# A third attention unit with a score buffer of its own, and a softmax tail that runs one weight tile later

## What is computed

```python
scores = einsum('bnqkgd,bnjkd->bnkgqj', qb, kb) * (HEAD_DIM ** -0.5)
scores = where(valid, scores, NEG_INF)              # causal, window of 128
m = maximum(max(scores, -1), sink)
pexp = exp(scores - m)
probs = pexp / (sum(pexp, -1) + exp(sink - m))
out = einsum('bnkgqj,bnjkd->bnqkgd', probs, vb)     # 8 heads, 2 key/value heads
branches = einsum('bsrc,rcd->bsrd', stack([y_conv, y_pool, y_att]), w_branch)
merged = sum(sigmoid(gate_logits) * branches, axis=2)
```

## Time and profile before

| | us |
|---|---|
| median of three runs | 1214.61 |
| the profiled execution: device time | 1214.84 |
| its span between first and last instruction | 1213.3 |
| TensorE busy in it | 1196.4 (99%) |
| VectorE busy | 887.0 (73%) |
| ScalarE busy | 715.4 (59%) |
| granted TensorE clock, mean share of full speed | 0.998 |
| first product of tile 14 of the gate stage, first layer | 172.81 |
| the same, second layer | 635.89 |

### The profile page before, as it was taken

The page is one execution under the profiler, slowest core; times in us unless marked ns, Lnnn a source line. Parts: engine busy times, 40 slices in busy tenths (PEclk is TensorE's granted clock), DMA queues, the critical chain, the costliest instruction groups (busy, mean ns, idle before and its releaser), DMA issues.

```text
span 1213.3 us, 15342 instructions
## 1 busy us (share of the span) xinstructions
PE 1196.4 (99%) x5990; PEld 997.6 (82%) x5990; DVE 887.0 (73%) x812; ACT 715.4 (59%) x675; POOL 111.4 (9%) x134
## 2 busy tenths in 40 slices
PE   8999999999999999999999999999999999999997
PEld 5998788888888888998788888888888888888875
DVE  4777755655444457767755788998888988888996
ACT  5437444543443437336534577777777777777765
POOL 3620000200000001340000000001000000000301
PEclk9999999999999999999999999999999999999999
DMA  9955455665555555555455499999999999999970
GB/s 333 323 196 176 163 181 175 220 217 188 181 200 176 191 188 174 191 174 174 145 171 186 150 359 371 387 374 389 378 388 380 392 377 390 380 389 378 393 286 35
DMA packets 152457, 319.11 MB, mean 263 GB/s; under 512 B 6000, under 2 KB 41088, under 8 KB 152400
## 3 DMA queue, kind: packets, MB, share of 16 engines
q1 hardware_dynamic: 147632, 302.80, 71.0%
q0 software_dynamic: 4480, 14.51, 3.2%
q10 hardware_dynamic: 288, 1.05, 0.3%
HBM read 311.51 MB, written 6.82 MB: 262 GB/s over the span
## 4 chain that ended last, share of the span: by engine, by line
PE 91%; DVE 4%; ACT 3%; issue 1%; DMA 1%; SPq 0%; POOLq 0%; DVEq 0%; POOL 0%; ACTq 0%
PE ps L1960 24%; PE ps L1705 17%; PE ps L1707 17%; PE ps L1706 17%; PE ps L1947 11%; DVE split L1057 2%; ACT split L674 1%; PE ps L1927 1%; PE ps L1721 1%; DMA raw<-ple_w_proj_dram 1%; PE ps L1772 1%; PE ps L1832 1%; PE ps L1904 1%; PE ps L1783 0%; DVE X L1278 0%
## 5 line engine op out<-in xcount | busy, mean ns | idle before, releaser
L1057 DVE TENSOR_TENSOR split<-raw,split 128x2048 fp32r<-128x2048 f32 x272 | 623.1, 2295 | 202.8 <-ACT split L674 200.3
L674 ACT ACTIVATE split<-raw 128x2048 fp32r<-128x2048 f32 x274 | 524.8, 1916 | 259.1 <-PE ps L1707 187.7
L1960 PE MATMUL ps<-split,br 128*128 128x512 f32 x1344 | 317.4, 392 | 0.5 <-DVE split L1057 0.3
L1960 PEld LDWEIGHTS ps<-split,br 128*128 128x128 f32 x1344 | 249.5, 188 | 54.9 <-DVE split L1057 2.0
L1705 PE MATMUL ps<-split,hT 128*128 128x512 f32 (+1 forms) x600 | 234.5, 391 | 2.5 <-DVE hT L1105 1.2
L1707 PE MATMUL ps<-split,hT 128*128 128x512 f32 (+1 forms) x600 | 230.4, 384 | 0.0
L1706 PE MATMUL ps<-split,hT 128*128 128x512 f32 (+1 forms) x600 | 230.3, 384 | 0.0
L1947 PE MATMUL ps<-split,hT 128*128 128x512 f32 x672 | 159.6, 392 | 0.1
L1947 PEld LDWEIGHTS ps<-split,hT 128*128 128x128 f32 x672 | 124.8, 188 | 27.9 <-issue 1.6
L1705 PEld LDWEIGHTS ps<-split,hT 128*128 128x128 f32 x600 | 112.8, 188 | 29.0 <-DVE hT L1105 3.3
L1707 PEld LDWEIGHTS ps<-split,hT 128*128 128x128 f32 x600 | 112.7, 188 | 22.5
(11 more groups left out here) (283 smaller groups left out, 963.1 us busy)
## 6 DMA issues: line engine op xcount, KB each, us to landing
raw<-moe_w_gu_dram SPq DMA_DIRECT2D x96, 1024.0 KB
raw<-moe_w_down_dram SPq DMA_DIRECT2D x56, 1024.0 KB
raw<-w_in_dram SPq DMA_DIRECT2D x45, 1024.0 KB
raw<-ffn_w_gu_dram SPq DMA_DIRECT2D x28, 1024.0 KB
raw<-moe_w_gu_dram SPq DMA_DIRECT2D x32, 512.0 KB
raw<-ffn_w_down_dram SPq DMA_DIRECT2D x14, 1024.0 KB
raw<-w_branch_dram SPq DMA_DIRECT2D x12, 1024.0 KB
raw<-w_out_dram SPq DMA_DIRECT2D x8, 1024.0 KB
```

Source lines behind the costliest of these rows:

```text
L674: act.activation(buffer(t, 0), raw[:, t % RAW, :], ACT.Copy).then_inc(hi, 1)
L1057: dve.tensor_tensor(buffer(t, 1), raw[:, t % RAW, :], buffer(t, 0).bitcast(F32), ALU.subtract).then_inc(lo, 1)
L1960: ins = pe.matmul(ps[:, 5 if kind == "up" else 4, :], xe[:, sl, 4 * part + k, :], slot(t, sr, 512)[:, k, :], start=part + k + m == 0, stop ...
```

## The change

It does four things.

1. `scores_of(2)` is no longer the first half of `Y` but `upool[:, :, 16:]`. With that the wait for `pr_turned` ahead of unit 2's mask goes. Since `upool` is not contiguous over heads, scores are now addressed by head.
2. The six turns move from after tiles 5 to 10 to after tiles 6 to 11, and the six copies (`take_probs`) from tiles 6 to 11 to tiles 7 to 12.
3. The three products with the values move from after tiles 7, 9, 11 to after tiles 8, 10, 12.
4. `ATT_HALF` becomes 9 and `ATT_OUT` 13: `values_hi` and `values_lo` also move one tile on.

```diff
@@ -38,7 +38,7 @@
 
 
 
-ATT, ATT_HALF, ATT_OUT = 1, 8, 12
+ATT, ATT_HALF, ATT_OUT = 1, 9, 13
 ATT_UNITS = ((0, 0, HEADS, P), (1, 0, HEADS // 2, SEQ), (1, HEADS // 2, HEADS // 2, SEQ))
 
 CHAN_COLS = (1536, 1792, 512, 768, 1024, 1280, 0, 256)
@@ -367,7 +367,9 @@
 
         def scores_of(u):
 
-            return Y[:, u % 2, :]
+            if u == 2:
+                return upool[:, :, 16:]
+            return Y[:, u, :].rearrange("p (h n) -> p h n", n=ATT_UNITS[u][3])
 
         def probs_of(half):
 
@@ -775,7 +777,7 @@
                 _, _, nh, n = ATT_UNITS[u]
                 act.wait_ge(masked, 3 * l + u + 1)
                 for h in range(nh):
-                    s = scores_of(u)[:, h * n:(h + 1) * n]
+                    s = scores_of(u)[:, h, :]
                     act.activation(s, s, ACT.Exp, bias=nmx[:, u % 2, h:h + 1],
                                    accum_out=den[:, u % 2, h:h + 1])
                 act.activation(esk[:, u % 2, 0:nh], esk[:, u % 2, 0:nh], ACT.Exp).then_inc(exped, 1)
@@ -1189,9 +1191,7 @@
             def mask_scores(l, u):
                 _, h0, nh, n = ATT_UNITS[u]
                 dve.wait_ge(s_done, 3 * l + u + 1)
-                if u == 2:
-                    dve.wait_ge(pr_turned, 6 * l + 2)
-                s3 = scores_of(u).rearrange("p (h n) -> p h n", h=nh)
+                s3 = scores_of(u)
                 for s in range(2):
                     ins = dve.scalar_tensor_tensor(
                         out=s3[:, s:nh:2, :],
@@ -1527,8 +1527,8 @@
                         at = 3 * c + step
                         if at == ATT_HALF:
                             values_lo(l, 0)
-                        if 0 <= at - ATT - 5 < 6:
-                            take_probs(l, at - ATT - 5)
+                        if 0 <= at - ATT - 6 < 6:
+                            take_probs(l, at - ATT - 6)
                         for stage, late in ((scale_probs, 4), (mask_scores, 1)):
                             if at - ATT - late in (0, 2, 4):
                                 stage(l, (at - ATT - late) // 2)
@@ -1776,12 +1776,14 @@
 
             def att_turn(l, piece):
                 u, half = piece // 2, piece % 2
+                per = ATT_UNITS[u][3] // P
                 pe.wait_ge(probs, 3 * l + u + 1)
                 if piece:
                     pe.wait_ge(prT_ready, 6 * l + piece)
                 for i in range(4):
                     ins = pe.transpose(ps[:, 7, i * P:(i + 1) * P],
-                                       scores_of(u)[:, (4 * half + i) * P:(4 * half + i + 1) * P], ident[:, :])
+                                       scores_of(u)[:, (4 * half + i) // per, i % per * P:(i % per + 1) * P],
+                                       ident[:, :])
                 ins.then_inc(pr_turned, 1)
 
             def att_values(l, u):
@@ -2175,10 +2177,10 @@
                                 if b == 0:
                                     ins.then_inc(branch_done, 1)
                         ins.then_inc(tile_used, 1)
-                        if at - ATT - 6 in (0, 2, 4):
-                            att_values(l, (at - ATT - 6) // 2)
-                        if 0 <= at - ATT - 4 < 6:
-                            att_turn(l, at - ATT - 4)
+                        if at - ATT - 7 in (0, 2, 4):
+                            att_values(l, (at - ATT - 7) // 2)
+                        if 0 <= at - ATT - 5 < 6:
+                            att_turn(l, at - ATT - 5)
                         if at - ATT in (0, 2, 4):
                             att_scores(l, (at - ATT) // 2)
                         if at == 15:
```

## The result

| | before | changed |
|---|---|---|
| median, us (12 runs each) | 1214.44 | 1217.86 |
| lowest to highest | 1213.97 to 1215.24 | 1216.05 to 1219.46 |
| profiled execution: span | 1213.3 | 1216.7 |
| TensorE busy | 1196.4 | 1197.9 |

The ratio is 1.0026, 95% interval 1.0019 to 1.0033: the change costs 3.4 us (2.3 to 4.0 by the interval), where 2.5 were forecast. The time is inside the range of 1215.3 to 1218.7, and 0.2 us above the narrower one, 1216.1 to 1217.7, that the forecast gave itself. Two things in the table were not forecast: almost a microsecond more, and runs of the changed kernel that spread over 3.4 us, those of before over 1.3.

The account below looks back on a forecast made before the run. TensorE, busy 99% of the span, was taken to bound the kernel. A 2.18 us loss less a 0.95 us gain per layer, 2.46 us over both, moved the median from 1214.61 to 1217.1 us; range 1215.3 to 1218.7.

Parts of the forecast that it names:

- the narrower one: Range for the main forecast alone, 1216.1 to 1217.7 us: the stall's bounds less 0.95 us, twice; chance 82%.
- What bounds the kernel: TensorE is busy 99% of the span, so only its standing still or doing more can move the end.
- The gain: Gate stage: without unit 2's mask wait, TensorE's waits for the `sc` copy and the division go, 0.95 us per layer.
- The loss: Tile 14: TensorE waits for `values_hi`, queued behind tile 13's second sigmoid, then `values_lo`; 2.18 us per layer.
- The sum: Whole kernel: 2.18 - 0.95 = 1.23 us slower in each layer, 2.46 in both, median 1217.1 us.
- the rival on the clock: Behind the new gap TensorE falls to 1.2 GHz for one tile, 5.5 us per layer, 1228 us; chance 3%.
- The chances: Whole kernel: slower 0.61, within 0.2% 0.37, faster 0.02.
- the edge at 0.2%: About 2.4 us, the least difference a measurement can tell from no change; the forecast lay there, at +0.20%.
- Nothing given back: Behind tile 14 TensorE has no standing wait that a later arrival could use up, so nothing was taken back.

Follow-up runs that it names:

- `hi_first`: Changed kernel with the values' high half issued at tile 13 ahead of the tile's two sigmoids: 1212.90 us against 1214.30, ratio 0.9987.
- `buffer_only`: Kernel before with only unit 2's scores in the pooling input's buffer and no wait ahead of its mask: 1212.26 us against 1214.30, ratio 0.9984.
- `before_out13`: Kernel before with only ATT_OUT moved from 12 to 13 (high and low half later): 1220.45 us against 1214.30, ratio 1.0046.
- `long_stall`: Changed kernel with the attention's last high half moved behind the next load's high half on ScalarE: 1224.23 us against 1214.39, ratio 1.0083.
- `again`: Changed kernel, unaltered, measured and profiled a second time against the kernel before: 1218.49 us, ratio 1.0035.
- `again2`: Changed kernel, unaltered, run for a third profile: 1218.29 us.
- `filled`: Changed kernel with seven matmuls that nothing reads laid into the gap at tile 14: 1217.30 us against 1214.39, ratio 1.0026.
- `out13_filled2`: Kernel before with ATT_OUT = 13 and seven matmuls that nothing reads at tile 14: 1219.50 us against 1214.83, ratio 1.0039.
- `long_filled2`: Changed kernel with the last high half behind the next load's, plus fourteen unread matmuls in the gap: 1221.08 us against 1214.83, ratio 1.0049.

## Why the prediction was right, and what it missed

- **What bounds the kernel.** Right: each wait of TensorE that came or went is found in the end time.
- **The gain, 0.95 us in each layer.** Right, measured 0.9 to 1.0 by `hi_first` and `buffer_only`. Of the change's parts only the buffer brings it.
- **The loss, 2.18 us in each layer.** The mechanism is as told, place by place, and shown by moving one copy (`hi_first`) and by moving it alone (`before_out13`). The time that TensorE loses there is 2.2 us.
- **The sum, 2.46 us.** The gate stages cost 2.6 us, the parts that the sum holds. The median moved by 3.4 us in one comparison and 4.2 in the other. The seven executions of the first comparison whose clock did not fall, by the table below, have a median 2.3 us above before; that is the case the sum was made for.
- **What was mis-sized: the rival on the clock.** It was given 3% and a price of a whole tile at half speed, 5.5 us in each layer. In truth it is neither all nor nothing. Behind a gap of 1.95 us the clock fell in two of eight gaps (the three profiles of the changed kernel and that of `before_out13`), and a fall cost 1.6 us, because seven or eight products, each 0.20 us longer, ran at half speed and not 24. The error was to read the earlier trace rows, where a gap of 1.17 us did no harm, as speaking for one of 2 us, and to treat the fall as a case of its own and not as a price of the stall with a chance in each execution. The Trainium skill ("TensorE: Matmul & The Clock Gate", section "HAM oscillation — how this bites in real kernels"), which the prediction had cited, tells of idle gaps, there waits for loads between groups of matmuls, that throw the engine back to the lower clock. The trace agrees that a gap can do so, with a granted clock down to 0.50 behind two gaps of 1.95 us and both of 3.74 us; here the wait was for VectorE, and the same gap did it in some cases only.
- **The chances.** 0.61 for slower was due, but that the time came clear of the edge at 0.2% was in part luck: the executions whose clock did not fall lie 2.3 us, or 0.19%, above before. With half a fall in the sum the forecast would have been about 1218, and the edge no question.
- **Nothing given back.** Right: from the end of a gate stage on, the difference to before stays within 0.2 us in all profiles.

How often the clock falls in executions without a profile can be read, with some care, from the mean granted clock that is on record for each. In the profiled executions it is 0.998 or 0.999 where no gap was followed by a fall, 0.997 with one fall and 0.994 in `long_stall`, with two, one of them longer. All executions of the kernels with a gap at tile 14, by this share:

| | at 0.998 or 0.999 | their median above before, us | at 0.997 or less | their median above before, us |
|---|---|---|---|---|
| changed kernel, first comparison | 7 | 2.3 | 5 | 3.9 |
| changed kernel, `again` | 2 | 3.1 | 4 | 4.4 |
| changed kernel, `again2` | 0 | | 1 | 3.9 |
| `before_out13` | 1 | 4.1 | 4 | 6.2 |
| `long_stall` | 0 | | 5 | 9.8 |
| `filled` | 10 | 2.9 | 1 | 4.2 |
| `out13_filled2` | 5 | 4.7 | 0 | |
| `long_filled2` | 5 | 6.3 | 0 | |

The 46 executions of the kernel before that these experiments were compared with and the 22 of `hi_first` and `buffer_only` are all at 0.998 or 0.999. So a fall is likely in 10 of 19 executions of the changed kernel, and those took 1.3 to 1.6 us more than the others of the same comparison. That is the part of the median that the sum had missed. The share is rounded and also holds what the clock does at the kernel's end, so that a single execution can be put in the wrong column. Open is why the same gap is followed by a fall in one execution and not in the next.

## What to carry to other kernels

An instruction that is moved later in a hand-written queue must be looked up by what stands ahead of it there, not by its tile number: here one copy of 0.6 us landed behind an instruction that waits for the end of the very tile whose successor needs the copy. If an edit takes away a wait, try it without the shifts that come with it; the shifts had no use here and cost more than the gain. A gap in the busiest engine's stream has to be priced with its clock afterwards, as a chance and not as an all-or-nothing case, and a kernel whose runs scatter more than before is a sign to look for it in more than one profile.

## What the hardware showed

- The same gap of 1.95 us was followed by full clock in six profiled cases and by half of it, 1.2 GHz, in two, for seven or eight products of 128x512 each time. A gap of about 3.7 us was followed by half clock in both of two cases, once for as many products and once for about twelve, at a cost of 2.5 us.
- Seven 128x128 products that nothing reads, laid into the 1.95 us gap, kept the clock at 1.00 in four gaps out of four (`filled`, `out13_filled2`), and fourteen did so in the long gap in two out of two, without making the chain longer. One execution of `filled` out of eleven still has a mean clock of 0.997.
- The wait on the attention's low half is listed as "issue", with no engine named, in every unfilled kernel that has it. With work laid into the gap, the rest of the same wait is listed with its engine (`DVE br L1188`; L1186 in `out13_filled2`).
